# Sums over gathered expert rows in a transformer trunk: from one expert per step across all tokens to one token per step across all experts

## The reference, cut to what matters

```
dot[e]  = h . U[expert[e]]                  for its 128 experts e
w[e]    = gate[e] * gelu(dot[e])
y       = sum over e of w[e] * V[expert[e]]
```

## Time and profile before

| what | value |
|---|---|
| median of 3 runs | 3099.57 us (3098.86 to 3105.06) |
| span of the profiled execution | 3171.6 us |
| PE, DVE, ACT, POOL busy | 2560 (81%), 2033 (64%), 884 (28%), 1459 (46%) us |
| DMA, mean over the span | 338 GB/s; 805 MB by POOL's gathers, 253 MB by SP's and ACT's queue |
| gathers issued | 1280, of which 256 are pairs of U and V |

### The profile page before, as it was taken

The page is one execution under the profiler, slowest core; times in us unless marked ns, Lnnn a source line. Parts: engine busy times, 40 slices in busy tenths (PEclk is TensorE's granted clock), DMA queues, the critical chain, the costliest instruction groups (busy, mean ns, idle before and its releaser), DMA issues. The chain is left out here.

```text
span 3171.6 us, 30406 instructions
## 1 busy us (share of the span) xinstructions
PE 2560.4 (81%) x8952; PEld 1459.0 (46%) x8952; DVE 2033.0 (64%) x4699; ACT 883.5 (28%) x2652; POOL 1459.4 (46%) x1284
## 2 busy tenths in 40 slices
PE   7899886978786769979997778888898777766666
PEld 3576633757553223356653224456666433232222
DVE  4522578876787884245448834677666888865665
ACT  1121123552222232144222211255412233222221
POOL 0000265554447775435456772555435344434442
PEclk9899998999988889988998899889899899989888
DMA  8757597979879999989999996988788799999996
GB/s 328 286 196 232 187 393 289 336 276 347 298 289 351 356 355 414 414 336 339 392 381 384 338 367 204 362 323 310 273 331 321 266 425 423 420 402 421 425 426 291
DMA packets 259362, 1071.04 MB, mean 338 GB/s; under 512 B 29440, under 2 KB 32256, under 8 KB 225664
## 3 DMA queue, kind: packets, MB, share of 16 engines
q0 software_dynamic: 184320, 805.39, 65.6%
q1 hardware_dynamic: 71712, 253.16, 21.3%
q10 hardware_dynamic: 3168, 10.55, 0.9%
HBM read 1065.67 MB, written 3.31 MB: 337 GB/s over the span
## 5 line engine op out<-in xcount | busy, mean ns | idle before, releaser
L782 PE MATMUL psum<-ring,wdiag 128*128 128x512 f32 x1396 | 727.3, 668 | 230.7 <-ACT wdiag L1074 153.8
L1752 POOL DMA_INDIRECT ring<-in_peer_u,experts x372 | 451.5, 1214 | 912.8 <-DVE dots L1309 442.2
L782 PEld LDWEIGHTS psum<-ring,wdiag 128*128 128x128 f32 x1396 | 285.6, 214 | 630.1 <-issue 577.0
L782 PE MATMUL psum<-work,wdiag 128*128 128x512 f32 x808 | 422.7, 668 | 168.3 <-ACT wdiag L1074 129.0
L1752 POOL DMA_INDIRECT ring<-in_peer_v,experts x410 | 448.2, 1093 | 230.4 <-issue 115.1
L1309 DVE CUSTOM_DVE_ANT_0 work<-work 128x1024 f32<-128x1024 f32 x270 | 326.6, 1226 | 127.6 <-DMA work<-in_peer_uv,experts 79.2
L1309 DVE CUSTOM_DVE_ANT_0 ring<-ring,work 128x1024 f32<-128x1024 f32 x242 | 292.7, 1225 | 139.0 <-DMA ring<-in_peer_uv,experts 90.3
L1309 DVE CUSTOM_DVE_ANT_0 ring<-ring,h2a 128x1024 f32<-128x1024 f32 x256 | 305.2, 1221 | 109.5 <-DMA ring<-in_peer_u,experts 103.9
L782 PEld LDWEIGHTS psum<-work,wdiag 128*128 128x128 f32 x808 | 161.7, 211 | 413.1 <-issue 395.8
L1065 ACT ACTIVATE acts<-dots 128x2 f32<-128x2 f32 x384 | 77.8, 203 | 930.1 <-DVE dots L1309 851.4
L872 PE MATMUL psum<-work,wring 128*128 128x256 f32 (+1 forms) x1760 | 329.7, 347 | 6.2 <-issue 5.7
(11 more groups left out here) (203 smaller groups left out, 2980.5 us busy)
## 6 DMA issues: line engine op xcount, KB each, us to landing
wring<-in_wpack SPq DMA_DIRECT2D x370, 512.0 KB
ring<-in_wpack SPq DMA_DIRECT2D x98, 512.0 KB, 6.3
ring<-in_peer_v,experts POOLq DMA_INDIRECT x410
ring<-in_peer_u,experts POOLq DMA_INDIRECT x372
work<-in_rows ACTq DMA_DIRECT2D x4, 1024.0 KB
wring<-in_wpack SPq DMA_DIRECT2D x16, 160.0 KB
work<-in_peer_u,experts POOLq DMA_INDIRECT x140
work<-in_peer_uv,experts POOLq DMA_INDIRECT x130
```

Source lines behind the costliest of these rows:

```text
L782: last = nc.tensor.matmul(psum[:, 6 + q, :], wdiag[:, SUM_NO[e] % SMALL, :], row("v", e)[:, 512 * q:512 * (q + 1)], start=(e % KSEL == 0), ...
L1752: pool.indirect_dma_start(dst, None, table, index).then_inc(got[ROW_SLOT[key]], 16)
```

## The change

The sum over V turns round. For one token POOL now gathers the V rows of its 128 experts, one expert a partition. The token's 128 weights are then a column, and the sum over experts is one contraction over the partitions. The matmul's stationary operand has 32 columns, 31 of them zero, so that the token's sum lands in its own row of a group of 32 PSUM partitions and zeros are added to the other 31 rows. Four tokens, one from each quarter of the tile, are taken in a step, each in its own column group of 32; a tile has 32 steps of 8 matmuls of 512 columns.

The stationary operands are windows into `z`, a buffer of zeros with one weight column at every 32nd place; ACT fills 16 tokens' columns with one copy (`zf`). The weights come from `gates` times gelu of the dots (`gm`, on DVE, for 32 experts at once) through a transpose (`xw`), and the indices of the V gathers from a transpose of the chosen experts (`xi`, `v_experts`). `acc` as a sum, `wdiag`, `fsum` and DVE's share of the sums go. The pairs of U and V go as well: every gather is 128 x 4 KB, 1536 in all.

Since a token's weights need all 128 dots, a tile's work has phases: 128 dots, then `turn` (last `gm`, `xw`, two fills), then 32 V steps. Tile 0's and tile 3's dots are dealt over the first half of the next stage, and their V steps over the second half and the first two groups of its `topk`. Tile 1's dots stand beside the `topk` of stage 1; its V steps and tile 2's dots beside the first 60% of stage 2, four dots to a step; tile 2's V steps beside the rest. Tile 4's dots stand beside the last `topk`; `turn(4)`, the V steps of tile 4 beside the dots of tile 5, and then `turn(5)` and tile 5's V steps stand behind all of it. The cells are one pool: each gather takes the one asked for longest ago, of 11 for tiles 0 and 3 and of 21 otherwise. POOL issues in the order in which dots and steps stand in `PROGRAM`.

```diff
-TIGHT, TOGETHER = (0, 3), (4, 5)
-V_LAG = 6
-U_SMALL, V_SMALL, U_MORE, V_MORE = 4, 7, 5, 5
+TIGHT = (0, 3)
+QUARTER = P // 4
+V_STEPS = QUARTER
+FILL = 4
+FILLS = V_STEPS // FILL
+Z_TOKENS = 2 * FILL * 4
+RINGS = 11
+MORE = 10
+def token_of(o):
+    return QUARTER * (o % 4) + o // 4
...
+def dots_of(n):
+    out = []
+    for k in range(KSEL):
+        out.append(("u", n, k))
+        if k % GROUP == GELU_LAG and k > GROUP:
+            out.append(("gm", n, k // GROUP - 1))
+    return out
+def turn(n):
+    return [("gm", n, HEAD_GROUPS - 1), ("xw", n), ("zf", n, 0), ("zf", n, 1)]
+def beside(dots, sums, lag):
+    out = dots[:lag]
+    rest = dots[lag:]
+    per = -(-len(rest) // len(sums))
+    for n, x in enumerate(sums):
+        out += x + rest[per * n:per * (n + 1)]
+    return out
...
+        dots = dots_of(n)
+        lay(dots[8 * (m > 0):], first, half)
+        set_(turn(n), half + 2)
+        last = PLACE[("topk", m + 1, 0, 2, 0)]
+        lay(sums_list(n, True), half + 3, last)
+        if m == 0:
+            one, two = dots_of(1), dots_of(2)
+            lay(one, PLACE[("topk", 1, 0, 1, 2)], PLACE[("begin", 2)])
+            b = PLACE[("begin", 2)]
+            done = PLACE[("topk", 2, 0, 2, 0)]
+            middle = part(b, done, 0.6)
+            lay(two[:6] + turn(1) + beside(two[6:], sums_of(1), 6) + finish_items(1), b, middle)
+            set_(turn(2), middle + 2)
+            lay(flat(sums_of(2)), middle + 3, done)
+            set_(dots_of(3)[:8], done + 1)
+        else:
+            lay(dots_of(4), PLACE[("topk", 3, 0, 1, 2)], end)
+            five = dots_of(5)
+            set_(five[:6] + turn(4) + beside(five[6:], sums_of(4), 6) + finish_items(4), end)
+            set_(turn(5) + flat(sums_of(5)) + finish_items(5), end)
...
+def row_cells():
+    cell, use, before, uses, last, when = {}, {}, {}, [0] * CELLS, [None] * CELLS, [-1] * CELLS
+    for at, key in enumerate(ASKS):
+        c = min(range(RINGS if key[1] in TIGHT else CELLS), key=lambda i: when[i])
...
-                        for q in range(2):
-                            last = nc.tensor.matmul(psum[:, 6 + q, :], wdiag[:, SUM_NO[e] % SMALL, :], row("v", e)[:, 512 * q:512 * (q + 1)],
-                                                    start=(e % KSEL == 0), stop=False)
-                        last.then_inc(rows_added, 1)
+                def add_rows(n, i):
+                    if i == 0 and n:
+                        pe.wait_ge(sums_free, n)
+                    if i % FILL == 0:
+                        pe.wait_ge(z_filled, FILLS * n + i // FILL + 1)
+                    for c in range(4):
+                        key = ("v", n, 4 * i + c)
+                        pe.wait_ge(got[ROW_CELL[key]], 16 * ROW_USE[key])
+                    for q in range(2):
+                        for c in range(4):
+                            o = 4 * i + c
+                            at = QUARTER * (o % Z_TOKENS + 1) - 1 - i
+                            last = nc.tensor.matmul(psum[QUARTER * c:QUARTER * (c + 1), 6 + q, :], z[:, at:at + QUARTER],
+                                                    row(("v", n, o))[:, 512 * q:512 * (q + 1)], start=(i == 0), stop=(i == V_STEPS - 1))
+                    last.then_inc(rows_added, 1)
...
-                            nc.scalar.activation(wdiag[:, d % SMALL, :], ident, ACT.Identity, scale=wts[:, e % SMALL:e % SMALL + 1])\
-                                .then_inc(diags_made, 1)
+                    if kind == "u" and it[2] % GROUP == GROUP - 1:
+                        g = it[2] // GROUP
+                        act.wait_ge(dots_ready, KSEL * n + it[2] + 1)
+                        d = dots[:, g * GROUP:(g + 1) * GROUP]
+                        nc.scalar.activation(d, d, ACT.Gelu).then_inc(gelu_ready, 1)
+                    elif kind == "xw":
+                        full(act, it)
+                        if n:
+                            act.wait_ge(z_filled, FILLS * n)
+                        taken(nc.scalar.copy(wts[:, :], bank(it)[:, 0:P]))
+                    elif kind == "zf":
...
+                        if FILLS * n + b >= 2:
+                            act.wait_ge(rows_added, FILL * (FILLS * n + b - 1))
+                        at = QUARTER - 1 + P * FILL * (b % 2)
+                        dst = z[:, at:at + P * FILL].rearrange("p (i c s) -> p i c s", i=FILL, c=4)[:, :, :, 0]
+                        src = wts[:, :].rearrange("p (c i) -> p i c", c=4)[:, FILL * b:FILL * (b + 1), :]
+                        nc.scalar.copy(dst, src).then_inc(z_filled, 1)
```

More of the change, by code:

```diff
@@ new lines, in flat, with part, lay, set_ @@
+def flat(groups):
+    return [x for g in groups for x in g]
+def part(first, last, share):
+    total, done = sum(cost(x) for x in WORK[first:last]), 0.0
+    for n in range(first, last):
+        done += cost(WORK[n])
+        if done >= total * share:
+            return n
+    return last
+def schedule():
+    at = {}
+    end = len(WORK)
+    def lay(items, first, last):
+        for x, place in zip(items, deal(first, last, items)):
+            at.setdefault(place, []).append(x)
+    def set_(items, place):
+        at.setdefault(place, []).extend(items)
+    for m in CONTEXT:
+        n = TILE_NO[(STAGES[m][0], 0)]
+        first = PLACE[("topk", 0, 0, 1, 3)] if m == 0 else PLACE[("begin", 3)] + 1
+        chosen = PLACE[("topk", m + 1, 0, 0, 0)]
+        half = part(first, chosen, 0.5)
+        dots = dots_of(n)
+        if m:
+            set_(finish_items(n - 1), PLACE[("begin", 3)])
+        lay(dots[8 * (m > 0):], first, half)
[17 more added lines that the diff above has]
+            set_(turn(5) + flat(sums_of(5)) + finish_items(5), end)
+    return at
@@ L394 @@
-VECTOR_SUM = vector_sums()
-def by_vector(e):
-    return VECTOR_SUM[e]
-SUM_NO, _sums = [], {True: 0, False: 0}
-for _e in range(ALL_EXPERTS):
-    SUM_NO.append(_sums[by_vector(_e)])
-    _sums[by_vector(_e)] += 1
-def sums_before(e, vector):
-    return sum(by_vector(i) == vector for i in range(e))
+ASKS = []
+for _x in PROGRAM:
+    if _x[0] == "u":
+        ASKS.append(_x)
+    elif _x[0] == "v":
+        ASKS += [("v", _x[1], 4 * _x[2] + _c) for _c in range(4)]
+def row_cells():
+    cell, use, before, uses, last, when = {}, {}, {}, [0] * CELLS, [None] * CELLS, [-1] * CELLS
+    for at, key in enumerate(ASKS):
+        c = min(range(RINGS if key[1] in TIGHT else CELLS), key=lambda i: when[i])
+        uses[c] += 1
+        cell[key], use[key], before[key] = c, uses[c], last[c]
+        last[c], when[c] = key, at
+    return cell, use, before
@@ L444, in evacuator @@
     return FIXED_BY[kind]
[L447 removed]
+NO_PSUM = ("begin", "macc", "norms", "outs", "ln1_rows", "ln1", "topk", "u", "gm", "zf", "v", "fin")
 ITEMS = [x for x in PROGRAM if x[0] not in NO_PSUM]
@@ L1734, in _ @@
                         next(choosing[it[1:4]])
+                    elif kind == "xi":
+                        t = tiles[it[2]]
+                        full(dve, it)
+                        taken(nc.vector.tensor_scalar(v_experts[:, t * P:(t + 1) * P], bank(it)[:, 0:P], cols[:, l, C_LO:C_LO + 1], None, ALU.add))
             @block.gpsimd
```

332 lines of the change are left out of this document (112 added, 220 removed).

## The result

The changed kernel takes 3274.11 us, median of 4 runs (3269.04 to 3275.26), against 3099.51 us for the kernel before on the same chip: ratio 1.055, 95% interval 1.0534 to 1.0566. The forecast was 3122 us with a range of 3000 to 3245. The larger of its chances was "slower", but the loss is 175 us where it had 23.

What follows compares the result with a forecast made beforehand. A chain hopping between PE, DVE and ACT was taken to pace two stretches, DMA the others. Terms -45 - 3 - 50 + 121 = +23 us made a span of 3195 us, times 0.977 = 3122 us; range 3000 to 3245.

Steps and rivals of the forecast that it cites:

- The V step: In the sum over V, a step of 16 instructions takes 1.9 us, 61 us per tile.
- a sign of being wrong: Wrong if V steps exceed 3 us, two stretches shrink over 60 us each, or the end runs at 400 GB/s throughout.
- (b): In the V steps, weight loads are not hidden: 4.3 us a step, 3242 us in all; chance 0.12.
- (c): In the V steps, column groups don't overlap at all: 6.9 us a step, 3492 us in all; chance 0.07.
- Stage 1 -45, stage 3 -50: One tile's experts beside latent work: gains of 45 us (370 to 931) and 50 us (1891 to 2492).
- credit side: In 1891 to 2492, the V sum's 11.2% of the chain, 67 us, goes; -18 us after 49 us of new steps.
- The second credit, U landing and issue: In 1891 to 2492, U rows get 11 cells instead of 4, giving back half of 57 us: -29 us.
- The middle, -3: 931 to 1891: about +20 us while stage 1 chooses, -23 us from there on; bounds -40 and +40.
- The end, +121: 2492 to the end: no V step runs beside the last topk, gathers come later; 3293 against 3171.6, bounds +84 and +140.
- POOL's cadence: After the last topk, 235 sets with a dot for every second one take 1.43 us each, 336 us.
- bound (d): At the end, POOL isn't the brake and tile 4's U rows suffice: +84 instead of +121, 3086 us; no separate chance.
- The factor 0.977: Whole kernel: median 3099.57 against profile span 3171.6, used to scale the forecast span 3195 to 3122 us.

Runs made afterwards that it cites:

- a_narrow: Changed kernel with the matmuls of V steps 1 to 30 over 64 of their 512 columns: 3202.68 us, ratio 1.0323.
- b_unpair_short: Kernel before with tiles 4 and 5 gathered as single rows and every dot over 64 of 1024 words: 3210.61 us, ratio 1.0155.
- b_unpair_narrow: Kernel before with tiles 4 and 5 unpaired and PE's sum matmuls over 64 of 512 columns save a tile's first: 3135.57 us, ratio 1.0106.
- a_few_matmuls: Changed kernel keeping one of eight V matmuls in steps 1 to 30 of each tile: 3316.27 us, ratio 1.0475.

## Why the prediction was wrong, point by point

**The V step: right at full clock.** PE's timeline of after at 3157 and 3162, one step each:

```profile
3157.37 1.92 PE L780 MATMUL psum<-ring,z 128*32 128x512 f32 x16 [1.62 <-DMA ring<-in_peer_v,v_experts]
3162.36 3.50 PE L780 MATMUL psum<-ring,z 128*32 128x512 f32 x16 [3.07 <-DMA ring<-in_peer_v,v_experts]
```

1.92 us for 16 instructions, where 1.9 was taken; one by one they would need 6.9 us. The next step takes 3.50 us, at half the clock. The mean step is 2.1 us in stage 1 (66 us of L780 for 32 steps, clock 0.85) and 3.1 us in 2775 to 3268 (201 us for 64, clock 0.67), over the 3 us that the prediction named as a sign of being wrong; it cost nothing there, since the end of a_narrow is as long (769 against 768 us). The four column groups run together, and the weight loads are hidden (28 ns each, 14.43 us for 512): rivals (b) and (c) are refuted. The Trainium skill (TensorE: Matmul & The Clock Gate, Part 3) gives 2.38 times for three column tiles; here four give 6.9 / 1.92 = 3.6 times. Its rule that a weight load passes a running matmul only when the row groups differ would have made a step longer; these rows don't show that.

**"Stage 1 -45, stage 3 -50": this is the step that failed.** Its cost side was right. The 49 us of V steps on the path are there: the chain of waits of after, 2200 to 2490, by line,

```profile
by line: PE psum L1029 19.5%; PE psum L870 19.5%; PE psum L780 17.2%; PE psum L1011 9.6%; PE psum L895 7.8%; PE psum L972 3.1%; PE psum L996 2.7%; PE psum L1039 2.6%; DVE stat L1282 1.8%; issue 1.4%; PE psum L982 1.4%; PE psum L844 1.3%; PO
```

has 17.2% of 290 = 50 us on L780. Its credit side was wrong: it took 67 us for the sum over V because that was its share of the chain. The share itself was stretched: it was read over 438 us, where it is 49 us, and applied to 601 us and to stage 1, for which the trace keeps no chain. And a share is not a gain. The experiment gives 0.6 us in stage 1 and 12 in stage 3 (573.7 against 585.8 from tile 2's sum to stage 3's first index) for most of PE's part, the slower clock included. DVE's part of the sum was not taken away by itself, and so it isn't shown what it was worth. The second credit, U landing and issue, did not come out as time either. The waits did fall as foretold (waits of after in 1930 to 2499, where the earlier trace rows has 203.1 and 56.1):

```profile
POOL ring L1750 <- PE psum L780: 170.4, 28, 14.7
POOL ring L1750 <- DVE dots L1298: 87.6, 11, 48.5
...
DVE ring L1298 <- DMA ring<-in_peer_u,experts: 12.6, 17, 1.7
```

DVE hardly waits for a U row any more, and stage 3's own work is only 17 us shorter. POOL now waits for V steps instead, and once 48.5 us for dots in the hole. A chain that hops between engines may be one of several of nearly the same length, so that taking a link out brings the next one; that is my reading, no run shows the other chains.

Two losses had no term. In stage 1, 27 us (147.4 against 120.6 us from first to last index of stage 0) are `topk` beside 74 dots instead of 36; from the last index of stage 0 on, stage 1 takes 454 us against 445. In front of stage 3, 40 us are the hole. In both PE stands still at `xi` until the last index (58.7 us at 516, 38.4 us at 1930), where the prediction let the `xi` transposes hide. That is a rival for part of these losses, and no run tests it.

**The middle, -3: off by 20, within its bounds of 40.** Stage 1's `topk` costs 30 us more where 20 were put, and the part behind it, full of bytes as said, gives 13 where 23 were put. The upper bound was added up wrongly: at 374 GB/s it is +29, not +40. Likewise PE without V is 294 us in the middle and not the 304 of rival (c). Neither changes the forecast.

**The end, +121: right in kind, +89 on a 3100 chip.** 149 sets were foretold beside stage 3's topk and 146 came; DVE was to be busy for 269 us and was for 262; the last index came 276 us after the first, where 278 was put. What was mis-sized is POOL's cadence: 1.43 us was taken for the part with dots. POOL's timeline of after there and, for comparison, in the topk stretch:

```profile
2905.98 0.94 POOL L1750 DMA_INDIRECT ring<-in_peer_u,experts  x1 [0.31 <-issue]
...
2614.18 1.77 POOL L1750 DMA_INDIRECT work<-in_peer_u,experts  x1 [0.31 <-issue]
```

With a dot for every second set the issue stays at 0.94 us and the cadence at 1.24; it is stretched where dots follow each other without a gap. That is bound (d) of the prediction, +84. On the 3164 chips the same term is 853.9 - 681.8 = +172 us, beyond every bound given, and the prediction's profile came from such a chip. The Trainium skill (GPSIMD Engine Reference, Specifications) says that GpSimd shares its SBUF interfaces with VectorE; the issue of 0.94 and 1.78 us agrees with that, and b_unpair_short shows that this isn't what single rows cost.

**The factor 0.977.** The profile stood 2.3% above the median, and the prediction spread that evenly. It was not even: a 3164 chip reaches stage 1's first index at 928.4 (929.0), then loses 70 us to tile 2's sum (1903.2 against 1832.7), 15 more up to stage 3's first index, and next to nothing at the end (681.8 against 678.6).

**What stays open.** Why the single rows of the changed kernel take 1.4 to 1.6 us a set at the end on 3164 chips and 1.24 on 3100 chips. It is not bytes, not the number of cells, not the dots alone; fewer V matmuls remove most of it. Nor is 1.24 us a rule of the 3100 chips: b_unpair_narrow takes 1.42 there (310 sets in 441 us behind its last index). What the nameless waits of 2 to 6 us are, the trace doesn't say. No run without the V matmuls but with the clock held up was made, and the two losses without a term were not tested on a 3100 chip.

## What to carry to other kernels

A share of the chain of waits is what a piece of work lies on, not what its removal gives: before it is credited, thin out just that work and see how far the next mark moves (here 71 us off the sum, 40 us off PE in all at its lower clock, gave 0.6). Look too for the places where an engine's order makes it wait for something new, here 38 us for the last expert index. When a sum is cut into phases, count the gathers that each stretch can still issue; those that find no cell or a full DVE come back later at the DMA's full rate, in this case 33 MB as 80 us. And when a profile's span isn't near the median of the runs, look for another kind of chip before scaling.

## What was not expected of the hardware

- Four column groups of 32 of an fp32 matmul run wholly together: 16 instructions in 1.92 us.
- Two kinds of chip: the kernel before 3100 and 3164 us, the changed one 3274 and 3361. The changed kernel, with single rows, differs most behind its last index (493 and 566 us), where the kernel before, with 8 KB pairs, doesn't (406 and 410).
- When work was taken from PE, its granted clock fell with it (0.91 to 0.82 in stage 1 of the kernel before), and the rest of its work took 32 us more, of the 71 us saved.
- PE can crawl with nothing to wait for: in a_few_matmuls the small matmuls of tile 4's finish, 0.37 us each, came one per 2.1 to 2.8 us from 3093 to 3126, behind waits that the trace puts down to issue, and went on so after the DMAs had gone idle at about 3113. That is most of the 40 us above; its cause was not found.
